# A precomputed row of expert changes in the block loop of a routed-experts stage

## The chip, the cores and the metric

The kernel runs on one core of one Trainium2 chip. The metric is the device time of one execution in microseconds (us), lower is better. Five engines work side by side on their own instruction streams: TensorE (PE, with its weight loads listed apart as PEld), VectorE (DVE), ScalarE (ACT), GpSimd (POOL) and SyncE (SP), which here only issues DMAs. They meet through semaphores. An engine's sequencer also carries out what is no tile work: waits, register arithmetic, branches, and loads of a register from memory. In the profile those carry a `q` behind the engine's name and do not count as busy.

## The reference, cut to what matters

One layer: a mixer (gated linear recurrences and chunked retention), then routed experts plus a shared expert, then a final norm. The change touches the experts alone:

```python
def swiglu(x, w_gate, w_up, w_down):
    return (jax.nn.silu(x @ w_gate) * (x @ w_up)) @ w_down

# each of 2048 tokens chooses 6 of 64 experts; tokens of one expert are packed
# into blocks of 128, every expert has at least one block
def run_block(args):
    tok, gw, e = args
    return swiglu(x[tok], w1[e], w3[e], w2[e]).astype(F32) * gw[:, None]
y = lax.map(run_block, (tok_buf, g_buf, block_expert))
routed = segment_sum(y, tok_buf)
out = routed + swiglu(x, ws1, ws3, ws2)
```

D_MODEL is 1024, the width of an expert 256, and everything is float32. How many blocks an expert has depends on the data.

## The kernel before, in words

Three stages follow each other: `front` and `mixer_out` (the mixer and the routing), `experts`, and `final`. The change lies in `experts` (from line 1826).

`experts` works through blocks of 128 tokens. Blocks 0 to 15 (NT = 16) are the shared expert over all tokens, written out in Python; blocks 16 and 17 are written out too; the rest runs in a hardware loop (`iterations`, `eng.Fori`) of two blocks a turn, on every engine. A block is a step `k`. The number of turns and the expert of a block are known only on the chip: `blocks_row` is a row of integers in on-chip memory (row 0: the expert of each block, 0 being the shared one; row 1 is filled, and nothing reads it), and `expert_of` loads one entry of it into a register (`value_load`, line 1937).

A float32 product is made of three passes with operands split into a high part (rounded by a copy on ScalarE) and a low part (the difference, on VectorE): hi x hi, hi x lo, lo x hi. So the weights of each expert have to be split as well: six pieces of 128 x 1024, four of gate and up (`split_gu` / `split`), two of down (`split_d`). The ring of raw and of split weights has two slots. The weights of expert e + 1 are split while e computes: pieces 0 to 2, then 3, in the first step of e, and the two down pieces in ScalarE's and VectorE's part `before` of the step after it. SP loads the raw pieces of expert e + 2 as soon as VectorE has split those of e (`load_free`), gate and up first, then down, in one strict order.

The order of a step `k` in the loop, engine by engine:

- PE (`step`, line 2364): gate and up, hi x hi; hi x lo; the two transposes of block k - 1's gated hidden (`ps_ht`); lo x hi; eight transposes of the gathered tokens of k + 1 (`ps_x`); then `down(k - 1)` into `ps_y`, which waits for the low part of the hidden (`ht_lo`).
- ACT (line 2136): two `change` calls, each with two `value_load`s; wait for the products of k - 1; pieces 0 to 2 if block k is the first of its expert; `copy_ht(k - 1)`; the down pieces if block k - 1 was a first one; tanh of k; `copy_xt(k + 1)`; piece 3 if k is a first one.
- DVE (line 2214): two `change` calls, four `value_load`s; pieces 0 and 1 if k is a first one; `copy_ht(k - 1)`; piece 2; gating; `copy_xt(k + 1)`; piece 3; the down pieces of `before`; `weigh(k - 1)`, which waits for the end of `down(k - 1)` (`d_done`) and multiplies `ps_y` by gate and gain.
- POOL (line 2052): gathers the tokens of k + 3 with an indirect DMA, and adds block k - 1 to the output rows in memory with an accumulating indirect DMA (`scatter`). Each scatter waits for the landing of the one before (`added`).

The order is written out by hand; no planner is involved. A "first" is computed as `(e - expert_of(k - 1)) * (NE - 1 - e)`, nonzero if the expert changed and is not the last.

Of the kernel before, what the change touches and what calls it, by code (L numbers as in the profile page):

```python
# [26 lines left out]
P = 128  # L27
# [44 lines left out]
def wait_apart(eng, semaphore, value):  # L72


    if not isinstance(value, int) or value > 0:
        eng.wait_ge(semaphore, value)
        eng.nop(nofuse=True)  # L77
# [1748 lines left out]
def experts(nc, for_dma, io, mod_d, h2_d, h2t_d, sum_d, list_d, ident, R, pre, pre_loaded, blocks_row, ends_row):  # L1826
# [12 lines left out]
    with ExitStack() as ctx:  # L1839
# [9 lines left out]
        def dma_sem(name):  # L1849
# [51 lines left out]
        sized, ordered = sem("sized"), sem("ordered")  # L1901
        block_row_done, ids_done, lists_turned, who_done, take_set, give_set = (
            sem(n) for n in "block_row_done ids_done lists_turned who_done take_set give_set".split())
        N_ROWS_DONE = 4
        added = dma_sem("added")
        clear(nc, semaphores)
        block = ctx.enter_context(nc.Block())
# [18 lines left out]
        def wait(eng, semaphore, value):  # L1926
            if not isinstance(value, int) or value > 0:
                eng.wait_ge(semaphore, value)
# [5 lines left out]
        def expert_of(eng, k):  # L1934
            if isinstance(k, int) and k <= NT:
                return int(k == NT)
            return eng.value_load(blocks_row[0:1, 0, bass.ds(k, 1)], min_val=0, max_val=NE - 1)

        def change(eng, k):

            if isinstance(k, int) and k <= NT:
                return expert_of(eng, k) + 1, k in (FIRST_SPLIT, NT)
            e = expert_of(eng, k)
            return e + 1, (e - expert_of(eng, k - 1)) * (NE - 1 - e)

        def at_change(eng, at, split, pieces):

            e, first = at
            if isinstance(first, bool):
                if first:  # L1950
                    for i in pieces:
                        split(e, i)
                return
            with eng.If(first):
                for i in pieces:
                    split(e, i)

# [143 lines left out]
        def _(act):  # L2101
# [29 lines left out]
            def copy_ht(k, par):  # L2131
                act.wait_ge(ht_done, k + 1)
                wait(act, d_done, k - 1)
                act.activation(h_t[0][:, par].bitcast(F32R), ps_t[:, 0:D_EXP], ACT.Copy).then_inc(ht_hi, 1)  # L2134

            def step(k, par, r):
                if isinstance(k, int) and k == NT + 1:
                    table(act)
                here = change(act, k)
                if not isinstance(k, int) or k > 0:  # L2140
                    before = change(act, k - 1)

                wait_apart(act, h_done, k)
                at_change(act, here, split_gu, range(3))
                if not isinstance(k, int) or k > 0:
                    copy_ht(k - 1, 1 - par)

                    wait_apart(act, d_done, k - 1)
                    at_change(act, before, split_d, range(N_GU, N_GU + N_D))
                act.wait_ge(h_done, k + 1)  # L2150
                wait(act, hg_done, k - 1)
                act.activation(th[:, par], ps_h[:, par, 0:D_EXP], ACT.Tanh, scale=0.5).then_inc(th_done, 1)  # L2152
                copy_xt(k + 1, 1 - par)
                at_change(act, here, split_gu, range(3, N_GU))
            copy_xt(0, 0)
            for i in range(N_GU):
                split_gu(0, i)
            for i in range(N_GU, N_GU + N_D):
                split_d(0, i)
            n = iterations(act, step)  # L2160
            copy_ht(n * 2 + (NT - 1), 1)

        @block.vector
        def _(dve):
# [34 lines left out]
                    c = slice(i * 512, (i + 1) * 512)  # L2199
                    dve.tensor_tensor(y[:, par, c], ps_y[:, i], g2[:, c], ALU.mult).then_inc(y_done, 1)  # L2200

            def weigh(k, par, r):

                if isinstance(k, int) and k < NT:
                    weigh_shared(k, par)
                    return
                wait(dve, added, (k - 1) * 16)
                dve.wait_ge(d_done, k + 1)
                for i in range(2):
                    c = slice(i * 512, (i + 1) * 512)  # L2210
                    dve.scalar_tensor_tensor(y[:, par, c], ps_y[:, i], gate[:, bass.ds(k, 1)], g2[:, c],  # L2211
                                             ALU.mult, ALU.mult).then_inc(y_done, 1)

            def step(k, par, r):
                if isinstance(k, int) and k == NT + 1:
                    table(dve)
                here = change(dve, k)
                before = change(dve, k - 1) if not isinstance(k, int) or k > 0 else None
                at_change(dve, here, split, range(2))
                if not isinstance(k, int) or k > 0:  # L2220
                    copy_ht(k - 1, 1 - par)
# [9 lines left out]
                if not isinstance(k, int) or k > 0:  # L2231
                    wait(dve, d_done, k - 1)
                    at_change(dve, before, split_d, range(N_GU, N_GU + N_D))
                    weigh(k - 1, 1 - par, None if r is None or (isinstance(k, int) and k == NT) else r - (1 - par))

            def sizes(tabs):

# [52 lines left out]
            def after(k):  # L2290
# [18 lines left out]
                if k == 7:  # L2309
                    dve.wait_ge(brow_done, 1)  # L2310

                    dve.tensor_copy(blocks_row[:].rearrange("p w (c k) -> p c w k", c=2),
                                    ps_r[0:1, :].rearrange("p (c w k) -> p c w k", c=2, w=2)).then_inc(rows_done, 1)
            copy_xt(0, 0)
            for i in range(N_GU):
                split(0, i)
            for i in range(N_GU, N_GU + N_D):
                split_d(0, i)
            n = iterations(dve, step, after)
            copy_ht(n * 2 + (NT - 1), 1)  # L2320
            weigh(n * 2 + (NT - 1), 1, n - 1)

        @block.tensor
        def _(pe):
# [200 lines left out]
```

## Time and profile before

| | us |
|---|---|
| median of 3 runs | 2784.51 (2784.37 to 2789.07) |
| the profiled execution | 2791.28 |
| its span, first to last instruction | 2789.4 |
| blocks 16 on (loop and its two steps ahead), span in the trace | about 1372 to 2735 |
| PE busy over the span | 2534.0 |
| DVE busy over the span | 1733.3 |
| ACT busy over the span | 1012.1 |

The profile is one execution. Busy times are sums over instructions. Waits are read from semaphore events, and each is put down to the engine whose event came last; "issue" stands for time in which the engine waited for nothing that the profile shows. The granted clock of TensorE over the span was 0.954 of full speed.

### The profile page before, as it was taken

How to read it: one execution, taken by the hardware profiler on the slowest of the kernel's cores; microseconds unless marked ns; L12 is line 12 of the kernel's file. 1: busy time of each engine (PE TensorE's matmuls, PEld its weight loads, DVE VectorE, ACT ScalarE, POOL GpSimd, SP SyncE). 2: the span in 40 equal slices, each digit the busy share in tenths (PEclk: the TensorE clock that was granted, in tenths of full speed). 3: DMA queues.
4: the chain of work that ended last, by engine and by line, in shares of the span. 5: the costliest groups of instructions: out<-in, count | busy, mean ns of one | idle time of the engine just before them, and what ended most of it. 6: DMA issues, size and time to landing. Idle time of an engine off the chain costs nothing. (4 is left out here: it accounts for less than half of the span.)

```text
span 2789.4 us, 51564 instructions
## 1 busy us (share of the span) xinstructions
PE 2534.0 (91%) x11959; PEld 2035.5 (73%) x11960; DVE 1733.3 (62%) x2732; ACT 1012.1 (36%) x1615; POOL 968.5 (35%) x1008
## 2 busy tenths in 40 slices
PE   8999999999929889849999999999999999999990
PEld 4787777776728777737887787777778777777870
DVE  4664564566325666655646757577785767768673
ACT  3221434332312222221324535254553435545352
POOL 1210025612234655531233333333333333333334
PEclk9999999999969998969999999999999999999995
DMA  7775758674565554336768969899897989979887
GB/s 280 299 274 192 267 199 301 218 282 162 190 222 200 170 166 165 119 108 165 202 173 256 265 178 284 238 265 296 242 300 189 277 256 272 292 193 289 253 233 273
DMA packets 239383, 641.94 MB, mean 230 GB/s; under 512 B 24268, under 2 KB 37904, under 8 KB 223824
## 3 DMA queue, kind: packets, MB, share of 16 engines
q1 hardware_dynamic: 188880, 459.75, 46.2%
q0 software_dynamic: 50432, 181.27, 26.9%
q8 instruction: 40, 0.66, 0.1%
q14 instruction: 31, 0.25, 0.0%
HBM read 463.61 MB, written 177.33 MB: 230 GB/s over the span
## 5 line engine op out<-in xcount | busy, mean ns | idle before, releaser
L2067 POOL DMA_INDIRECT sum_d<-w_shared_raw,give x136 | 236.7, 1741 | 647.5 <-DMA sum_d<-w_shared_raw,give 300.6
L2169 DVE TENSOR_TENSOR w_exp_lo<-w_exp,w_exp_hi (+1 forms) x256 | 307.7, 1222 | 95.5 <-ACT w_exp_hi L2108 78.4
L2337 PE MATMUL ps_h<-w_exp_hi,x_exp_t_hi 128*128 (+1 forms) x1216 | 312.8, 399 | 24.6 <-ACT w_exp_hi L2108 21.5
L2108 ACT ACTIVATE w_exp_hi<-w_exp (+1 forms) x256 | 258.5, 1054 | 179.9 <-issue 117.0
L2337 PE MATMUL ps_h<-w_exp_hi,x_exp_t_lo 128*128 (+1 forms) x1216 | 321.8, 407 | 0.0
L2337 PE MATMUL ps_h<-w_exp_lo,x_exp_t_hi 128*128 (+1 forms) x1216 | 310.5, 397 | 0.0
L2337 PEld LDWEIGHTS ps_h<-w_exp_hi,x_exp_t_hi 128*128 128x128 f32 x1216 | 229.2, 189 | 83.0 <-ACT w_exp_hi L2108 21.7
L1134 PE MATMUL ps_p<-wa_hi,hx_split 128*128 128x512 f32 x1088 | 278.9, 402 | 4.6 <-DVE kvqg_out L100 3.3
L2337 PEld LDWEIGHTS ps_h<-w_exp_lo,x_exp_t_hi 128*128 128x128 f32 x1216 | 229.7, 189 | 56.2
L2337 PEld LDWEIGHTS ps_h<-w_exp_hi,x_exp_t_lo 128*128 128x128 f32 x1216 | 217.7, 189 | 41.4
L2134 ACT ACTIVATE h_exp_t_hi<-ps_ht 128x256 fp32r<-128x256 f32 x152 | 58.1, 382 | 510.6 <-PE ps_ht L2346 502.6
L1134 PEld LDWEIGHTS ps_p<-wa_hi,hx_split 128*128 128x128 f32 x1088 | 205.4, 190 | 51.5 <-DVE kvqg_out L100 4.0
L2337 PE MATMUL ps_y<-w_exp_hi,h_exp_t_hi 128*128 (+1 forms) x608 | 205.9, 420 | 37.6 <-DVE h_exp_t_lo L2189 36.7
L2211 DVE SCALAR_TENSOR_TENSOR w_shared_raw<-ps_y,gate,g_row 128x512 f32<-128x512 f32 x272 | 191.0, 743 | 70.0 <-PE ps_y L2337 53.0
L2337 PE MATMUL ps_y<-w_exp_hi,h_exp_t_lo 128*128 (+1 forms) x608 | 193.8, 400 | 0.0
L2337 PE MATMUL ps_y<-w_exp_lo,h_exp_t_hi 128*128 (+1 forms) x608 | 193.5, 400 | 0.0
L2057 POOL DMA_INDIRECT w_shared_raw<-h_d,take x139 | 146.2, 1052 | 115.0 <-POOL take L2055 99.7
L2183 DVE TENSOR_TENSOR x_exp_t_lo<-ps_x,x_exp_t_hi 128x512 fp32r<-128x512 f32 x274 | 175.6, 682 | 0.0
L2189 DVE TENSOR_TENSOR h_exp_t_lo<-ps_ht,h_exp_t_hi 128x256 fp32r<-128x256 f32 x152 | 64.0, 421 | 148.4 <-ACT h_exp_t_hi L2134 134.3
L2337 PEld LDWEIGHTS ps_y<-w_exp_hi,h_exp_t_hi 128*128 128x128 f32 x608 | 105.9, 190 | 67.2 <-issue 46.9
L2174 DVE TENSOR_TENSOR w_exp_lo<-w_exp,w_exp_hi (+1 forms) x130 | 153.0, 1218 | 0.0
L2226 DVE SCALAR_TENSOR_TENSOR h_gated<-tanh_e,ps_h 128x256 f32<-128x256 f32 x152 | 63.6, 418 | 142.1 <-ACT tanh_e L2152 136.8
(294 smaller groups left out, 4434.9 us busy)
## 6 DMA issues: line engine op xcount, KB each, us to landing
w_exp<-in_experts SPq DMA_DIRECT2D x386, 512.0 KB
hx_split<-hx_d SPq DMA_DIRECT2D x54, 1024.0 KB, 5.4
rec_m<-rec_d SPq DMA_DIRECT2D x16, 1536.0 KB, 6.9
hx_d<-hx_split SPq DMA_DIRECT2D x18, 1024.0 KB, 6.1
wm_rest<-in_w_mod_rest POOLq DMA_DIRECT2D x16, 1024.0 KB, 5.8
rec_d<-kvqg_out SPq DMA_DIRECT2D x48, 256.0 KB, 4.3
xt<-in_xt POOLq DMA_DIRECT2D x18, 512.0 KB, 9.0
rec_d<-kt_kvf_out SPq DMA_DIRECT2D x32, 256.0 KB, 4.5
```

Of the source, the lines that this page charges most:

```text
L1134: last = pe.matmul(ps_p[:, s % 2], hx0[:, at, x, k].bitcast(F32R), wa[w][:, k, p % 2 * HD:(p % 2 + 1) * HD].bitcast(F32R), start=(m + k == ...
L2057: pool.indirect_dma_start(xg[:, par], None, h2_d[:, :], bass.IndirectOffsetOnAxis(take[:, par:par + 1], 0)).then_inc(gathered[par], 16)
L2067: pool.indirect_dma_start(sum_d[:, :], bass.IndirectOffsetOnAxis(give[:, par:par + 1], 0), y[:, par], None, compute_op=ALU.add).then_inc(a ...
L2108: act.activation(w[0][:, piece(e, i)].bitcast(F32R), raw(e, i), ACT.Copy).then_inc(gu_hi, 1)
L2134: act.activation(h_t[0][:, par].bitcast(F32R), ps_t[:, 0:D_EXP], ACT.Copy).then_inc(ht_hi, 1)
L2169: dve.tensor_tensor(w[1][:, piece(e, i)].bitcast(F32R), raw(e, i), w[0][:, piece(e, i)], ALU.subtract).then_inc(gu_lo, 1)
L2174: dve.tensor_tensor(w[1][:, piece(e, i)].bitcast(F32R), raw(e, i), w[0][:, piece(e, i)], ALU.subtract).then_inc(wd_lo, 1)
L2183: dve.tensor_tensor(x_t[1][:, par, c].bitcast(F32R), src, x_t[0][:, par, c], ALU.subtract).then_inc(xt_lo, 1)
L2189: dve.tensor_tensor(h_t[1][:, par].bitcast(F32R), ps_t[:, 0:D_EXP], h_t[0][:, par], ALU.subtract).then_inc(ht_lo, 1)
L2211: dve.scalar_tensor_tensor(y[:, par, c], ps_y[:, i], gate[:, bass.ds(k, 1)], g2[:, c], ALU.mult, ALU.mult).then_inc(y_done, 1)
L2226: own.of(dve.scalar_tensor_tensor(hg[:, par], th[:, par], 1.0, ps_h[:, par, 0:D_EXP], ALU.add, ALU.mult))
L2337: last = pe.matmul(out, x[:, j * P:(j + 1) * P].bitcast(F32R), w_part[:, bass.ds(w_at + j * stride, 512)].bitcast(F32R), start=(start and ...
```

## The change

A row of what changes at each block is made once, on VectorE after step 7: with `turn[k]` = e + 1 if block k is the first of its expert and the expert is not the last, else 0, entry k of row 1 of `blocks_row` is `turn[k - 1] * 128 + turn[k]`. ACT and DVE load this one entry a step and take it apart by `% P` and `// P` (P = 128). A zero means: nothing to split. Two more increments of `rows_done` come with it (one replaces the old one), so `N_ROWS_DONE` is 5.

The order of the loop's bodies also turns: on ACT the tanh of k - 1 and `copy_xt(k)` stand at the head of step k, behind the load, and with them piece 3 of `before`; on DVE `weigh(k - 2)` stands at the head of step k, behind the load. What was at the end of one step is at the beginning of the next, and the last ones follow the loop. PE, POOL and SP are as they were; PE still loads its own expert number twice a step.

```diff
-        N_ROWS_DONE = 4
+        N_ROWS_DONE = 5
...
-        def change(eng, k):
+        def changes(eng, k):
             if isinstance(k, int) and k <= NT:
-                return expert_of(eng, k) + 1, k in (FIRST_SPLIT, NT)
-            e = expert_of(eng, k)
-            return e + 1, (e - expert_of(eng, k - 1)) * (NE - 1 - e)
+                return tuple((0 if j not in (FIRST_SPLIT, NT) else 1 if j == FIRST_SPLIT else 2) for j in (k, k - 1))
+            both = eng.value_load(blocks_row[0:1, 1, bass.ds(k, 1)], min_val=0, max_val=NE * P - 1)
+            return both % P, both // P
...
+            def gated(k, par):
+                act.wait_ge(h_done, k + 1)
+                wait(act, hg_done, k - 1)
+                act.activation(th[:, par], ps_h[:, par, 0:D_EXP], ACT.Tanh, scale=0.5).then_inc(th_done, 1)
...
-                here = change(act, k)
+                here, before = changes(act, k)
                 if not isinstance(k, int) or k > 0:
-                    before = change(act, k - 1)
-                wait_apart(act, h_done, k)
+                    gated(k - 1, 1 - par)
+                    copy_xt(k, par)
+                    at_change(act, before, split_gu, range(3, N_GU))
                 at_change(act, here, split_gu, range(3))
...
                     at_change(act, before, split_d, range(N_GU, N_GU + N_D))
-                act.wait_ge(h_done, k + 1)
-                wait(act, hg_done, k - 1)
-                act.activation(th[:, par], ps_h[:, par, 0:D_EXP], ACT.Tanh, scale=0.5).then_inc(th_done, 1)
-                copy_xt(k + 1, 1 - par)
-                at_change(act, here, split_gu, range(3, N_GU))
...
-                here = change(dve, k)
-                before = change(dve, k - 1) if not isinstance(k, int) or k > 0 else None
+                here, before = changes(dve, k)
+                if not isinstance(k, int) or k > NT:
+                    weigh(k - 2, par)
                 at_change(dve, here, split, range(2))
...
-                    weigh(k - 1, 1 - par, None if r is None or (isinstance(k, int) and k == NT) else r - (1 - par))
+                if isinstance(k, int) and 0 < k < NT:
+                    weigh(k - 1, 1 - par)
...
-                    dve.tensor_copy(blocks_row[:].rearrange("p w (c k) -> p c w k", c=2),
-                                    ps_r[0:1, :].rearrange("p (c w k) -> p c w k", c=2, w=2)).then_inc(rows_done, 1)
+                    of_block = blocks_row[:, 0]
+                    tabs.of(dve.tensor_copy(of_block.rearrange("p (c k) -> p c k", c=2),
+                                            ps_r[0:1, :].rearrange("p (c w k) -> p c w k", c=2, w=2)[:, :, 0]))
+                    turn, last = room[0:1, 0:2 * P], slice(1, 2 * P)
+                    tabs.of(dve.memset(turn, 0.0))
+                    tabs.of(dve.tensor_tensor(turn[:, last], of_block[:, last], of_block[:, 0:2 * P - 1], ALU.subtract))
+                    tabs.of(dve.scalar_tensor_tensor(turn, of_block, float(NE - 1), turn, ALU.is_lt, ALU.mult))
+                    tabs.of(dve.scalar_tensor_tensor(turn, of_block, 1.0, turn, ALU.add, ALU.mult))
+                    dve.tensor_copy(blocks_row[:, 1, 0:1], turn[:, 0:1]).then_inc(rows_done, 1)
+                    dve.scalar_tensor_tensor(blocks_row[:, 1, last], turn[:, 0:2 * P - 1], float(P), turn[:, last],
+                                             ALU.mult, ALU.add).then_inc(rows_done, 1)
```

## Rows read from the trace of the kernel before

**Rows 1.** The page: busy time, share and instructions of two engines.

```profile
PE 2534.0 (91%) x11959; PEld 2035.5 (73%) x11960; DVE 1733.3 (62%) x2732; ACT 1012.1 (36%) x1615; POOL 968.5 (35%) x1008
```

**Rows 2.** By stretch: length; PE, PEld, DVE, ACT, POOL busy; clock, DMA share, GB/s.

```profile
1900.00:2150.00 250.00, 244.11 (x1165) 197.03 (x1164) 178.00 (x249) 115.39 (x174) 88.07 (x101) 1.00 0.89 261
```

**Rows 3.** Waits of PEld, 1400 to 2720 us: total, times, longest.

```profile
PEld ps_y L2337 <- issue: 42.9, 53, 2.6
PEld ps_h L2337 <- issue: 4.7, 8, 0.8
```

**Rows 4.** Waits of PE matmuls, the same stretch.

```profile
PE ps_y L2337 <- DVE h_exp_t_lo L2189: 30.4, 36, 2.4
```

**Rows 5.** Timeline, an even pace: two starts of a step.

```profile
2413.55 1.83 PEld L2337 LDWEIGHTS ps_h<-w_exp_hi,x_exp_t_hi 128*128 128x128 f32 x8
...
2423.08 1.83 PEld L2337 LDWEIGHTS ps_h<-w_exp_hi,x_exp_t_hi 128*128 128x128 f32 x8
```

**Rows 6.** Timeline, one step that is the first of an expert: start, duration.

```profile
1448.61 1.83 PEld L2337 LDWEIGHTS ps_h<-w_exp_hi,x_exp_t_hi 128*128 128x128 f32 x8
...
1449.21 1.41 DVE L2211 SCALAR_TENSOR_TENSOR w_shared_raw<-ps_y,gate,g_row 128x512 f32<-128x512 f32 x2 [1.36 <-PE ps_y L2337]
1449.93 2.96 ACT L2108 ACTIVATE w_exp_hi<-w_exp  x3 [3.05 <-issue]
...
1453.01 0.39 ACT L2134 ACTIVATE h_exp_t_hi<-ps_ht 128x256 fp32r<-128x256 f32 x1
1453.22 2.36 DVE L2169 TENSOR_TENSOR w_exp_lo<-w_exp,w_exp_hi  x2 [2.60 <-ACT w_exp_hi L2108]
1454.45 1.03 PEld L2331 LDWEIGHTS ps_x<-ident,w_shared_raw 128*128 128x128 f32 x8
...
1455.50 0.42 DVE L2189 TENSOR_TENSOR h_exp_t_lo<-ps_ht,h_exp_t_hi 128x256 fp32r<-128x256 f32 x1
...
1456.31 0.32 PEld L2337 LDWEIGHTS ps_y<-w_exp_hi,h_exp_t_hi 128*128 128x128 f32 x2 [0.83 <-issue]
...
1458.99 0.19 PEld L2337 LDWEIGHTS ps_h<-w_exp_hi,x_exp_t_hi 128*128 128x128 f32 x1
```

**Rows 7.** Register loads of line 1937, DVE and PE, 1400 to 2720: ns min/median/max.

```profile
L1937 DVEq TENSOR_LOAD <-blocks_row x532: 297/310/1545, 1401.7 to 2712.4; - x178
...
L1937 PEldq TENSOR_LOAD <-blocks_row x266: 296/303/1382, 1405.0 to 2718.0; - x133
```

**Rows 8.** Timeline, the fourth of four first steps in a row.

```profile
2403.28 2.35 DVE L2174 TENSOR_TENSOR w_exp_lo<-w_exp,w_exp_hi  x2
...
2405.56 1.40 DVE L2211 SCALAR_TENSOR_TENSOR w_shared_raw<-ps_y,gate,g_row 128x512 f32<-128x512 f32 x2
...
2406.88 2.34 DVE L2169 TENSOR_TENSOR w_exp_lo<-w_exp,w_exp_hi  x2
```

**Rows 9.** Waits of PEld in two windows: 1734.9 to 1758.8, 2560.6 to 2581.6.

```profile
PEld ps_y L2337 <- issue: 3.5, 2, 2.6
...
PEld ps_y L2337 <- issue: 1.9, 2, 1.0
```

**Rows 10.** Timeline around the table of step 7, and a small operation of step 5.

```profile
1287.69 0.23 DVE L2276 TENSOR_TENSOR prod<-cmp,expert_steps 128x65 f32<-128x65 f32 x1
...
1303.56 0.67 DVE L2312 CAST blocks_row<-ps_rank 1x512 int32<-1x512 f32 x1
1306.64 0.42 DVE L2189 TENSOR_TENSOR h_exp_t_lo<-ps_ht,h_exp_t_hi 128x256 fp32r<-128x256 f32 x1 [2.41 <-ACT h_exp_t_hi L2134]
```

**Rows 11.** Timeline, ACT in a step with down pieces, block after a first one.

```profile
2418.78 2.01 ACT L2112 ACTIVATE w_exp_hi<-w_exp  x2 [0.44 <-issue]
...
2420.96 1.07 ACT L2128 ACTIVATE x_exp_t_hi<-ps_x 128x512 fp32r<-128x512 f32 x2
```

**Rows 12.** Waits of POOL and DVE for the scatters, 1400 to 2720 us.

```profile
POOL sum_d L2067 <- DMA sum_d<-w_shared_raw,give: 300.6, 58, 7.3
...
DVE w_shared_raw L2211 <- DMA sum_d<-w_shared_raw,give: 8.2, 6, 1.4
```

More of the change, by code:

```diff
@@ L1937, in expert_of, with at_change @@
             return eng.value_load(blocks_row[0:1, 0, bass.ds(k, 1)], min_val=0, max_val=NE - 1)
-        def change(eng, k):
+        def changes(eng, k):
             if isinstance(k, int) and k <= NT:
-                return expert_of(eng, k) + 1, k in (FIRST_SPLIT, NT)
-            e = expert_of(eng, k)
-            return e + 1, (e - expert_of(eng, k - 1)) * (NE - 1 - e)
[L1946 to L1950, printed above, removed]
+                return tuple((0 if j not in (FIRST_SPLIT, NT) else 1 if j == FIRST_SPLIT else 2) for j in (k, k - 1))
+            both = eng.value_load(blocks_row[0:1, 1, bass.ds(k, 1)], min_val=0, max_val=NE * P - 1)
+            return both % P, both // P
+        def at_change(eng, e, split, pieces):
+            if isinstance(e, int):
+                if e:
                     for i in pieces:
@@ L1953, in at_change @@
                 return
-            with eng.If(first):
+            with eng.If(e):
                 for i in pieces:
@@ L2160, in _ @@
             n = iterations(act, step)
+            gated(n * 2 + (NT - 1), 1)
+            copy_xt(n * 2 + NT, 0)
             copy_ht(n * 2 + (NT - 1), 1)
@@ L2200, in weigh_shared, with weigh @@
                     dve.tensor_tensor(y[:, par, c], ps_y[:, i], g2[:, c], ALU.mult).then_inc(y_done, 1)
-            def weigh(k, par, r):
+            def weigh(k, par):
                 if isinstance(k, int) and k < NT:
@@ L2319, in _ @@
             n = iterations(dve, step, after)
+            weigh(n * 2 + (NT - 2), 0)
             copy_ht(n * 2 + (NT - 1), 1)
-            weigh(n * 2 + (NT - 1), 1, n - 1)
+            weigh(n * 2 + (NT - 1), 1)
         @block.tensor
```

## The prediction

> **What bounds the kernel now.** I read the page first: PE is busy 91% of the span [rows 1], so a change on the other engines can only give back time in which PE stands still. The table by stretch says the same of the block loop: PE 244.1 of 250 us, at a granted clock of 1.00, which is the 2.4 GHz level, and with the DMA engines at a share of 0.89 [rows 2]. The reader is to see two things there: PE's idle time is a few per cent, and DMA has little room.
>
> How much PE idles depends on the row one trusts. The waits of PEld in the loop are 42.9 us in 53 gaps ahead of `ps_y`, the down product, and 4.7 us ahead of `ps_h` [rows 3]; the waits of the matmuls themselves are only 30.4 us [rows 4]. I took the timeline to decide. Steps without a change of expert start 2423.08 - 2413.55 = 9.53 us apart [rows 5], and every such step looks the same. A step that is the first of its expert took 1458.99 - 1448.61 = 10.38 us [rows 6], 0.85 more, and the PEld gap in it is 0.83. So PEld's gaps are what a step loses, and the loop loses 42.9 + 4.7 = 47.6 us: the ceiling of the change. The Trainium skill ("Perfetto Trace Analysis", Per-instruction lifecycle) says that the profiler estimates where a TensorE instruction ends rather than observing it; here the trace agrees, the matmul row being short by 12 us, and by that row the sum below would be some 10 us smaller.
>
> Then, what is late in such a step? With PE's step start at 1448.61 [rows 6]: the transposes of `ps_x` are through at 1455.48, and `down` then stands until DVE's `h_exp_t_lo` (1455.50 to 1455.92). That copy is behind the two split pieces on DVE (1453.22 to 1455.58), its input from ACT was ready at 1453.40. The splits begin 2.60 us after DVE had finished `weigh` at 1450.62. The row blames ACT's `w_exp_hi`, but ACT made those from 1449.93 on, three in 2.96 us, so the first was ready at about 1450.9. What lies in the gap are the four register loads on DVE's sequencer: 532 over 133 steps, 0.31 us each by median [rows 7]; 4 x 0.31 = 1.24 us, and the arithmetic and range checks that the view of line 1937 has between them fill the rest, so that a load costs about 2.60 / 4 = 0.65 us with them. DVE's queue has nothing in it meanwhile. So the wait that ends last is the sequencer's own, and it lies between `weigh` and the splits.
>
> The Trainium skill ("Advanced Engine Details and Errata", Sequencer Loop) speaks against this reading: other engine instructions can be read and queued while the sequencer's microcode works on a control instruction. By it the loads would cost nothing, and the change would give 0. The row disagrees: the 2.60 us hold no tile work, with raw and high parts there. What the code shows is why: the splits stand in an `If` whose condition is made of the loads.
>
> **The change part by part.** Removed on DVE: three of four loads a step, and the fourth goes ahead of `weigh`'s wait for `d_done`. In [rows 6] DVE had 1.36 us idle ahead of `weigh`, waiting for PE; one load with its arithmetic is about 0.65 us, and with the turn of the loop about 1.1 us by an estimate, so it fits in. Then the splits can start when `weigh` ends, +2.0 us into the step, and end at +4.4. `h_exp_t_hi` is ready at +4.8, the low part at +5.3, and PE asks for it only at +6.87. The stall of such a step goes to zero with 1.6 us to spare; what is late next is PE itself, at 9.53 us a step. That the high pieces are there at +2.0 needs ACT earlier too: its three loads fewer and the fourth ahead of tanh let pieces 0 to 2 follow `copy_xt`, so they start 2 to 3 us earlier than 1449.93; even unmoved the first is ready at +2.3.
>
> This holds for first steps that do not follow two others. Where three or four experts of one block stand in a row, DVE has more than a step of work: six pieces at 2.35 / 2 = 1.17 us each, `weigh` 1.40, and with both copies and the gating some 2.5 more, nearly 11 us by an estimate from [rows 6, 8]. There the splits follow `weigh` with no gap (2405.56 + 1.40 against 2406.88), and `weigh` follows the down pieces (2403.28 + 2.35 against 2405.56) [rows 8]. No load is on that path, so those stalls stay. The wait view over the last two steps of each of the six such rows gives 3.5 us in the first and 1.9 in the last [rows 9], with 2.4, 2.1, 2.6 and 2.6 in between: 15.1 us. It contains the places where weight DMAs land late. The 4.7 us ahead of `ps_h` [rows 3] stay too: PE waits there for its own two loads a step, which take up to 1.38 us [rows 7] and are not touched.
>
> Sum: 42.9 - 15.1 = 27.8 us of stall that a load gates. From both sides: at most all 47.6; at least what only the pure case gives. Long loads are part of the 27.8: DVE's maximum is 1.545 us [rows 7], and four chances a step become one, ahead of a wait.
>
> Added: the table in step 7. One cast of 0.67 us becomes seven operations that each wait for the one before. The small ones of step 5 take 0.16 to 0.23 us [rows 10] for 65 elements; for 256 I take 0.4, with the wait, 7 x 0.4 = 2.8 us, 2.1 more than now. Behind the cast DVE idles 2.41 us for ACT's copy [rows 10], so 0; if that cover were gone, 2.1 us at most. Once, not per step.
>
> Moved: ACT's load now stands ahead of tanh. In a step with down pieces ACT works until 2418.78 + 2.01 = 2420.79, and tanh and `copy_xt` follow at once [rows 11]; the sequencer is free from the moment at which it handed over the second down piece, some 1 us earlier. A load with arithmetic and the loop's turn is 0.6 to 1.1 us, as on DVE, so tanh is between nothing and 0.2 us late; `copy_xt` ends at 2422.03 and PE takes its tile at 2423.08 [rows 5, 11], 1.05 us of cover. A load as long as the longest of DVE's, 1.545 us against 0.31 [rows 7], passes the cover by 0.2 to 0.4. I take 0; the far end, such a load in each of the 53 stalled steps, is 53 x 0.4 = 21 us, and the median is near the short end. `weigh`, the scatter and the gathers keep their order on their engines; the ends of the loop have the same order as before, so 0 there, give or take 0.5.
>
> Given back: the stretches with many changes get 2 to 3% faster, with DMA at 0.89. Scatters run one at a time; 58 were released by the landing of the one before [rows 12], and DVE's `weigh` waited for a scatter 8.2 us in 6 places. Saving some 1 us per pair of first steps lets such waits come up more often: I take 1 us from the sum, between 0 and 10.
>
> The forecast is 27.8 - 1 = 26.8, say 27 us. Against the profiled execution it is 2791.3 to 2764; that execution is 6.8 us above the median of the runs shown, and a span with 2 us around it. The predicted median is 2784.5 - 27 = 2757.5.
>
> **The rivals.**
>
> A: the time comes back as DMA waits. For it: the share of 0.89 [rows 2], 58 scatters bound to their predecessor [rows 12], and weights of the fourth expert in a row landing after they are wanted. Against: outside the rows of three and four PE's gaps are explained by the loads alone, and issue moves forward along with the splits. Half of the 27 would be left: 2771.
>
> B: no change. Either the load in its new place is as long as before on the same path, or the splits are late for another reason just behind it (ACT's high parts, should their loads still gate them). Against it are ACT's pieces of [rows 6], ready before the gap ends. 2784.5, within 5.
>
> C: slower, through the scatters. Place: POOL's accumulating DMA, one after another. Splits that come 2.5 us earlier put the weight loads for the next expert but one on the DMA engines 2.5 us earlier, on top of the scatter of `weigh`. POOL waits 300.6 / 58 = 5.2 us each for those of today [rows 12]. If each such scatter took a quarter of that longer, 1.3 us, and the backlog of every second one reached the loop, that is 29 x 1.3 = 38 us against the 27: 2795. It decides from the point at which a scatter lands later than two steps less a `weigh`, 2 x 9.53 - 1.40 = 17.7 us, behind its own `weigh` [rows 5, 8], since `y` has two buffers; at present DVE waits beyond it 8.2 / 6 = 1.4 us each, in 6 places.
>
> **How the numbers follow.** Forecast 0.72, A 0.14, B 0.07, C 0.07. Forecast and A are faster by over 0.2% (5.6 us, about what a measurement can tell from no change): 0.86. B is the same, 0.07; C slower, 0.07. The range: the forecast's own is from a gain of 38 (the stalls of the rows of four shrink by half too) to one of 17; A reaches to 2780. 2746 to 2780 leaves out B, C and little else.
>
> **What would show it.** The step of [rows 6] would take 9.53 us, and the DVE gap of 2.60 us ahead of its splits be under 0.3. PEld ahead of `ps_y` would sum to 14 to 18 us in the loop in place of 42.9, nearly all in third and fourth first steps, and ahead of `ps_h` 3 to 6. Loads of line 1937's kind would number about 134 on DVE and on ACT, and still 266 on PE. PE's step 8 would start on time. The prediction is wrong if gaps ahead of DVE's splits stay; if gaps ahead of `ps_h` grow (ACT's tanh and `copy_xt` late); or if DVE's waits for the scatter rise from 8 us to 20 and more.

## The result and the profile after

| | us |
|---|---|
| before, median of 4 runs | 2784.44 (2776.15 to 2789.07) |
| after, median of 4 runs | 2750.42 (2748.32 to 2753.66) |
| ratio | 0.9882, 95% interval 0.9856 to 0.9908 |
| the profiled execution after, and its span | 2748.32, 2746.5 |

The change makes the kernel 34.0 us faster; 27 were forecast, in a range from 2746 to 2780 us, which is a gain of 4.5 to 38.5. (Gains in microseconds are differences of medians, here and below, unless a ratio is named. The ratios are those on record and differ from the quotient of the medians by up to 0.0015.) The page of the kernel after, busy time of each engine (answers to [rows 1]):

```profile
PE 2512.4 (91%) x11959; PEld 2026.6 (74%) x11960; DVE 1743.4 (63%) x2738; ACT 1010.7 (37%) x1615; POOL 976.4 (36%) x1008
```

The same stretch as in [rows 2], with the same columns:

```profile
1900.00:2150.00 250.00, 247.22 (x1188) 201.48 (x1186) 180.72 (x252) 114.04 (x174) 87.14 (x102) 0.99 0.89 262
```

PE is busy 3.1 us more of the 250 and issues 23 more matmuls in them, at the same clock level and the same DMA share: the same work, closer together.

The waits in the block loop of the kernel after (engine, what it waited for, then total, times and longest; they answer to [rows 3, 12]):

```profile
POOL sum_d L2066 <- DMA sum_d<-w_shared_raw,give: 297.9, 61, 6.9
...
DVE w_shared_raw L2213 <- issue: 17.4, 20, 1.9
PEld ps_y L2351 <- issue: 15.5, 13, 2.8
...
DVE w_shared_raw L2213 <- DMA sum_d<-w_shared_raw,give: 5.7, 6, 1.4
...
DVE w_exp_lo L2171 <- ACT w_exp_hi L2107: 3.2, 10, 0.4
...
ACT w_exp_hi L2107 <- issue: 0.2, 1, 0.2
```

Ahead of `ps_y` 53 gaps have become 13. A row for `ps_h` is gone altogether. The two rows on scatters are as they were, so nothing came back there. The last row was 117.0 us before: ACT's high pieces no longer wait for its loads.

Where the 34 us lie: I measured the block loop as the distance from the first to the last of its steps' `ps_x` transposes, 136 steps. At 9.53 us a step that would be 1296 us; it was 1346.4 before and is 1313.0 after. The loop gained 33.4 us, the size of the median's gain. The two profiled executions differ by 9.6 us more, ahead of the loop, where the change has nothing (the second shared block starts at 1235.0 in one and at 1225.4 in the other), which is a difference between executions.

The step of [rows 6], the same block, in the timeline of the kernel after (start, duration):

```profile
1438.96 1.83 PEld L2351 LDWEIGHTS ps_h<-w_exp_hi,x_exp_t_hi 128*128 128x128 f32 x8
...
1439.52 1.41 DVE L2213 SCALAR_TENSOR_TENSOR w_shared_raw<-ps_y,gate,g_row 128x512 f32<-128x512 f32 x2 [1.23 <-PE ps_y L2351]
...
1440.84 2.35 DVE L2171 TENSOR_TENSOR w_exp_lo<-w_exp,w_exp_hi  x2
...
1443.78 0.42 DVE L2191 TENSOR_TENSOR h_exp_t_lo<-ps_ht,h_exp_t_hi 128x256 fp32r<-128x256 f32 x1 [0.59 <-ACT h_exp_t_hi L2133]
...
1445.81 0.30 PEld L2351 LDWEIGHTS ps_y<-w_exp_hi,h_exp_t_hi 128*128 128x128 f32 x2
...
1448.49 0.19 PEld L2351 LDWEIGHTS ps_h<-w_exp_hi,x_exp_t_hi 128*128 128x128 f32 x1
```

It takes 1448.49 - 1438.96 = 9.53 us in place of 10.38. The splits follow `weigh` with no gap where 2.60 us lay, the copy of the hidden's low part (0.42 us) starts 4.82 us into the step in place of 6.89, and `ps_y` comes without a gap.

The 13 gaps that are left, two of them in the timeline, the third and fourth of four first steps in a row:

```profile
2527.37 0.32 PEld L2351 LDWEIGHTS ps_y<-w_exp_hi,h_exp_t_hi 128*128 128x128 f32 x2 [0.87 <-issue]
...
2539.70 0.32 PEld L2351 LDWEIGHTS ps_y<-w_exp_hi,h_exp_t_hi 128*128 128x128 f32 x2 [2.77 <-issue]
```

All 13 lie in such rows, as in [rows 9]. Seven are 0.85 to 0.88 us; five are longer, to 2.77, and one is 0.23.

The register loads after (ns min/median/max) answer to [rows 7], and the table in step 7 to [rows 10]:

```profile
L1943 ACTq TENSOR_LOAD <-blocks_row x135: 273/279/820, 1367.2 to 2661.9; - x135
...
L1943 DVEq TENSOR_LOAD <-blocks_row x135: 300/317/1628, 1371.7 to 2667.1; - x135
...
L1937 PEldq TENSOR_LOAD <-blocks_row x270: 296/303/1517, 1369.1 to 2674.6; - x135
...
1293.92 0.40 DVE L2317 CAST blocks_row<-ps_rank 1x256 int32<-1x256 f32 x1
...
1296.14 0.40 DVE L2325 SCALAR_TENSOR_TENSOR blocks_row<-prod 1x255 int32<-1x255 f32 x1
1297.00 0.42 DVE L2191 TENSOR_TENSOR h_exp_t_lo<-ps_ht,h_exp_t_hi 128x256 fp32r<-128x256 f32 x1 [0.46 <-ACT h_exp_t_hi L2133]
```

One load a step on ACT and on DVE, two still on PE (these counts are over the whole trace, 135 steps with loads). The table takes 1296.54 - 1293.92 = 2.62 us, and the copy behind it still waits for ACT.

### The profile page after: what moved, and what is told of

Same layout as the page of the kernel before. It is cut to its first block and busy times, and to the rows that moved or that the text cites. A ratio compares the mean times of both kernels' runs of the same rounds, so it can differ in the third digit from the quotient of the medians.

```text
span 2746.5 us, 47753 instructions
## 1 busy us (share of the span) xinstructions
PE 2512.4 (91%) x11959; PEld 2026.6 (74%) x11960; DVE 1743.4 (63%) x2738; ACT 1010.7 (37%) x1615; POOL 976.4 (36%) x1008
## 5 line engine op out<-in xcount | busy, mean ns | idle before, releaser
L2066 POOL DMA_INDIRECT sum_d<-w_shared_raw,give x136 | 237.8, 1749 | 624.3 <-DMA sum_d<-w_shared_raw,give 297.9
L2351 PE MATMUL ps_y<-w_exp_hi,h_exp_t_hi 128*128 (+1 forms) x608 | 205.2, 419 | 18.5 <-DVE h_exp_t_lo L2191 15.2
L2127 ACT ACTIVATE x_exp_t_hi<-ps_x 128x512 fp32r<-128x512 f32 x274 | 148.4, 595 | 2.1
```

What stands on the lines that cost most here:

```text
L2066: pool.indirect_dma_start(sum_d[:, :], bass.IndirectOffsetOnAxis(give[:, par:par + 1], 0), y[:, par], None, compute_op=ALU.add).then_inc(a ...
L2127: act.activation(x_t[0][:, par, b * 512:(b + 1) * 512].bitcast(F32R), ps_x[:, b], ACT.Copy).then_inc(xt_hi, 1)
L2351: last = pe.matmul(out, x[:, j * P:(j + 1) * P].bitcast(F32R), w_part[:, bass.ds(w_at + j * stride, 512)].bitcast(F32R), start=(start and ...
```

## The experiments

**The theory:** the 42.9 us ahead of `ps_y` were DVE's four loads behind `weigh`; one load ahead of it removes them, and the order of the bodies matters little beside the number of loads. **Rivals:** the order is what pays, since it puts the load ahead of a wait; or ACT's loads are what pays. Two more questions came from the trace after: why the `ps_h` gaps went, and what holds the 15.5 us that are left.

The kernel before takes another time from one group of runs to the next (medians of 2760.59, 2762.41 and 2783.96), so only ratios within a group are compared. The last three columns are from the profiled execution.

| | median, us | before beside it | ratio (95%) | loop, us | ahead of `ps_y` | ahead of `ps_h` |
|---|---|---|---|---|---|---|
| e1, the row alone | 2733.99 | 2760.59 | 0.9894 (0.9874 to 0.9914) | 1319.6 | 18.5 | 1.5 |
| e2, the order alone | 2818.35 | 2760.59 | 1.0198 (1.0176 to 1.022) | 1401.9 | 73.2 | 29.9 |
| e3, both on DVE alone | 2732.67 | 2760.59 | 0.9896 (0.9874 to 0.9917) | 1316.1 | 16.8 | 4.9 |
| e4, both on ACT alone | 2766.01 | 2760.59 | 1.0015 (0.9999 to 1.0032) | 1349.8 | 46.3 | 5.4 |
| e5, SP's order too | 2728.86 | 2762.41 | 0.9864 (0.9843 to 0.9886) | 1308.1 | 10.5 | 2.5 |
| e6, after again | 2731.94 | 2762.41 | 0.9891 (0.987 to 0.9913) | 1308.7 | 12.6 | 0 |
| e7, after, four loads on PE | 2750.26 | 2762.41 | 0.9959 (0.994 to 0.9978) | 1336.5 | 7.8 | 44.6 |
| e8, before, four loads on PE | 2799.35 | 2762.41 | 1.0134 (1.0109 to 1.0159) | 1381.7 | 19.5 | 79.5 |
| e9, less of DVE's splits | 2741.06 | 2783.96 | 0.9853 (0.9838 to 0.9868) | 1305.2 | 0 | 9.1 |
| e10, a split on POOL | 2760.8 | 2783.96 | 0.9927 (0.9914 to 0.9941) | 1322.4 | 21.7 | 4.1 |
| e11, e5 again | 2745.55 | 2783.96 | 0.9858 (0.9844 to 0.9872) | 1307.3 | 10.6 | 1.5 |

### e1: the row alone

Table and single load as in the change; the bodies in the old order (against the kernel after).

```diff
                 here, before = changes(act, k)
-                if not isinstance(k, int) or k > 0:
-                    gated(k - 1, 1 - par)
-                    copy_xt(k, par)
-                    at_change(act, before, split_gu, range(3, N_GU))
+                wait_apart(act, h_done, k)
                 at_change(act, here, split_gu, range(3))
...
+                gated(k, par)
+                copy_xt(k + 1, 1 - par)
+                at_change(act, here, split_gu, range(3, N_GU))
...
                 here, before = changes(dve, k)
-                if not isinstance(k, int) or k > NT:
-                    weigh(k - 2, par)
                 at_change(dve, here, split, range(2))
...
-                if isinstance(k, int) and 0 < k < NT:
+                if not isinstance(k, int) or k > 0:
                     weigh(k - 1, 1 - par)
...
```

> The row and its one load a step on both engines, but the loops' bodies in the old order: the load lies where the four loads lay, between weigh and the split pieces on VectorE. Theory (the loads' length gates the splits): one load with its arithmetic and branches is about 1.0 us in place of 2.6, so the splits start about +3.0 us into the step, before the +3.7 at which the copy of the hidden's low part begins to be late; PEld ahead of ps_y 15 to 20 us in the loop, 27 to 33 us faster than before, within 3 us of the full change. Rival (it is the place that counts, the load must be ahead of the wait for down): the splits remain gated, PEld ahead of ps_y 25 us and more, half the gain or less (0 to 17 us).

0.9894 is a gain of 29.3 us at its group's 2760.6 (26.6 by the medians), and e6 has 0.9891: within the intervals the row alone is the whole change. In the profile the loop is some 6 to 11 us longer than in the kernel after (1319.6 against 1313.0 and 1308.7), with 3 to 6 us of it ahead of `ps_y`. What the order adds is at most a few us.

DVE's waits ahead of the splits that follow `weigh`, in the loop of the kernel before and then of e1:

```profile
DVE w_exp_lo L2169 <- ACT w_exp_hi L2108: 78.4, 42, 3.3
...
DVE w_exp_lo L2169 <- issue: 16.3, 10, 3.8
...
DVE w_exp_lo L2181 <- ACT w_exp_hi L2119: 8.6, 23, 0.8
DVE w_exp_lo L2181 <- issue: 7.6, 34, 1.4
```

94.7 us have become 16.2, with the one load still behind `weigh`. Directly behind `weigh`, counted over the 62 first steps of the loop, the gap was 1.53 us by mean before and is 0.14 in e1, with 0.15 at most in 42 of them and 1.41 at the longest. A look at DVE's sequencer in the step of [rows 6] tells why so little is left:

```profile
L1937 DVEq TENSOR_LOAD <-blocks_row x4: 299/302/325, 1449.8 to 1451.9; - x4
```

The first load starts at 1449.8, while `weigh` is still at work (to 1450.62), because the sequencer goes on as soon as it has handed `weigh` over. So the beginning of a chain of loads hides behind `weigh`, and a short chain hides nearly whole. What e1 doesn't part is the load itself from the arithmetic, the check and the branch that go with it: the row removes all of them together.

### e2: the order alone

The new order of the bodies with the old `change`, four loads a step (against the kernel after).

```diff
-                here, before = changes(act, k)
+                here = change(act, k)
+                before = change(act, k - 1) if not isinstance(k, int) or k > 0 else 0
...
-                here, before = changes(dve, k)
+                here = change(dve, k)
+                before = change(dve, k - 1) if not isinstance(k, int) or k > 0 else 0
```

> The new order with four loads a step at the head of the step, ahead of tanh on ScalarE and of weigh on VectorE. Theory: on VectorE 2.6 us of loads begin 1.4 us before down ends, weigh is about 1 us late and the splits start near +3.0: no stall from VectorE. On ScalarE the loads end 2.7 us after the hand-over of the last copy, later than the end of the gate and up products, so tanh and the token copy are 1 us late in plain steps (covered) and 1 to 2 us late in steps with down pieces (cover 1.05 us): gaps ahead of ps_h appear, 10 to 40 us in all. Net between 20 us faster and 10 us slower than before. Rival (place is all that counts): as fast as the full change, no gaps ahead of ps_h.

It is 58 us slower than before: the order doesn't pay by itself. My expectation, 10 us slower at most, missed this by far. The waits of its loop:

```profile
ACT tanh_e L2150 <- issue: 159.6, 96, 2.8
DVE w_shared_raw L2226 <- issue: 143.3, 80, 4.5
DVE w_shared_raw L2226 <- DMA sum_d<-w_shared_raw,give: 124.4, 45, 4.4
...
PEld ps_y L2365 <- issue: 73.2, 63, 2.5
...
PEld ps_h L2365 <- issue: 29.9, 49, 2.7
```

The first two rows have "issue" as what was waited for: the engine's own sequencer. Four loads with their arithmetic are some 2.6 us, and now tanh and `weigh` stand behind them in every step, not in first steps alone. ACT's tanh becomes late 96 times, `weigh` 80 times. The third row is the late `weigh` passed on: scatters start later, one behind another, and the next `weigh` finds its buffer still in use. With one load (the row of the kernel after above) `weigh` is late 20 times and by 17.4 us in all, which no PE row shows. So the order is safe only with the row. No run has the four loads ahead of tanh alone or ahead of `weigh` alone, so how the 58 us are shared between ACT and DVE is open.

### e3 and e4: one engine at a time

e3 has the new loads and order on DVE and the old ones on ACT; e4 the other way round. e3's edit against the kernel before:

```diff
             def step(k, par, r):        # DVE
-                here = change(dve, k)
-                before = change(dve, k - 1) if not isinstance(k, int) or k > 0 else None
+                here, before = changes(dve, k)
+                if not isinstance(k, int) or k > NT:
+                    weigh(k - 2, par)
...
```

> VectorE as in the full change, ScalarE with its four loads in the old place. Theory (the path is VectorE's): 27 to 33 us faster than before, since ScalarE's first piece is ready +2.3 us into the step and VectorE can begin at +2.0; the gap ahead of VectorE's splits is 0.3 to 0.5 us. Rival (ScalarE's late pieces gate as well): half of that, with VectorE's idle time ahead of its splits of 1 us and more, put down to ScalarE rightly.

> ScalarE as in the full change, VectorE with its four loads in the old place. Theory: within 4 us of the kernel before; ScalarE's pieces come 2 to 3 us earlier and wait, VectorE's gap of 2.6 us stays, PEld ahead of ps_y 38 to 43 us. Rival (ScalarE gates): 10 us faster and more.

DVE alone gives the whole gain (0.9896), ACT alone none (1.0015, with 1 in the interval). e4's waits:

```profile
DVE w_exp_lo L2183 <- issue: 99.6, 52, 3.7
...
PEld ps_y L2361 <- issue: 46.3, 52, 2.7
```

In e3 ACT still waits for its loads (117.0 us before), and DVE waits for ACT:

```profile
ACT w_exp_hi L2119 <- issue: 138.4, 51, 4.4
...
DVE w_exp_lo L2182 <- ACT w_exp_hi L2119: 24.7, 40, 1.9
```

DVE's 24.7 us in 40 places are ACT's late high pieces; directly behind `weigh` the gap is 0.37 us by mean over the 62 first steps, as expected. Little of it reaches PE: e3 has 16.8 + 4.9 us of gaps, the kernel after 15.5, and the loop of e3 is 3.1 us longer. So ACT's loads are a second wait, just behind DVE's own, and the path is DVE's.

e4 also corrects the reading of [rows 6]: with ACT's high pieces early, the row ahead of DVE's splits no longer blames ACT but "issue", 99.6 us in 52 places. The wait was the sequencer's all along, as the prediction had it from the sum of the loads.

### e6, e7 and e8: more loads on PE

e6 is the kernel after again, beside the others. e7 and e8 add two loads a step to PE, in the kernel after and before.

```diff
             def step(k, par, r):        # PE
+                if not isinstance(k, int):
+                    for _ in range(2):
+                        expert_of(pe, k)
                 e = expert_of(pe, k)
```

> The full change as it is, timed beside the others on one chip, for its gain with a smaller interval: 31 to 36 us faster than before.

> The full change, and TensorE's sequencer loads its expert number twice more at the head of each step (four loads a step in place of two). My prediction held that the 4.7 us ahead of ps_h are TensorE's own slow loads and stay; they went to 0 though slow loads on TensorE did not get fewer. Theory: where down is not late the sequencer is ahead of the array by more than a load, so that even 1.3 us more of loads a step hide: within 4 us of the full change. Rival (the loads are on the path, and luck took the slow ones away): 134 steps with 1.3 us more, 20 us and more slower than the full change.

> The kernel before with the same two extra loads on TensorE. Theory (a late down uses up the lead of TensorE's sequencer, then the loads at the head of the next step show): gaps ahead of ps_h in most of the steps in which down was late, 53 of them, up to 1 us each: 10 to 50 us slower than before, where the same loads cost the full change next to nothing. Rival (independent of the stall): the same cost in both kernels.

These ask why the `ps_h` gaps went although PE's loads were not touched. My expectation for e7 was under 4 us; it cost 18.3 (2750.26 - 2731.94), nearer to the rival's "20 us and more", and e8 36.9 (2799.35 - 2762.41). e7's loop:

```profile
PEld ps_h L2351 <- issue: 44.6, 68, 1.3
```

PE's sequencer runs ahead of the array, and a load is hidden as long as that lead lasts. Two loads fit in, four fit in half of the steps. The lead is consumed when `down` was late, since the sequencer then stood at that wait and has nothing queued behind it. The two traces show it step by step (counting `down` as late where PEld stood for over 0.12 us ahead of it): behind a late `down` every step has a gap ahead of `ps_h`, of 1.11 us by mean in e7 (8 steps) and 1.20 in e8 (32 steps); behind one on time 60 of 128 steps have one in e7, of 0.59 us, and 53 of 104 in e8, of 0.78. So e8 loses twice what e7 does. (The loop of e7 is 27.8 us longer than e6's and its gaps 39.8 us more, so a gap of PEld ahead of `ps_h` isn't lost to the full.) The gaps of the kernel before answer to the same reading. One of its cases, a step whose `down` is late, with the load that follows, in the view of line 1937 and in the timeline:

```profile
L1937 PEldq TENSOR_LOAD <-blocks_row x1: 1107/1107/1107, 2380.1 to 2380.1; - x1
...
2378.65 0.32 PEld L2337 LDWEIGHTS ps_y<-w_exp_hi,h_exp_t_hi 128*128 128x128 f32 x2 [0.86 <-issue]
...
2381.97 1.70 PEld L2337 LDWEIGHTS ps_h<-w_exp_hi,x_exp_t_hi 128*128 128x128 f32 x8 [0.67 <-issue]
```

And a longer load in the kernel after, in a step whose `down` was on time:

```profile
L1937 PEldq TENSOR_LOAD <-blocks_row x1: 1297/1297/1297, 1531.8 to 1531.8; - x1
...
1533.76 0.43 PEld L2351 LDWEIGHTS ps_y<-w_exp_hi,h_exp_t_lo 128*128 128x128 f32 x2
1534.23 0.90 PEld L2351 LDWEIGHTS ps_h<-w_exp_hi,x_exp_t_hi 128*128 128x128 f32 x4
```

Before, 1107 ns behind a late `down` left a gap of 0.67 us; after, 1297 ns left none. I counted PE's loads of over 0.6 us that stand between a `down` and the next `ps_h`. In the kernel before, 8 were behind a late `down` and gave the row's 8 gaps, and 6 behind one on time gave none. e4 has 8 with 8 gaps and 6 with 2 (each in the step after a stalled one). After, all 18 were behind a `down` on time and gave none. Over the ten traces with two loads a step, e2 aside, it is 20 gaps for 21 loads behind a late `down`, and 9 for 137 behind one on time. The kernel after still has 13 late ones, and that no long load met one of them is in part luck: at the rate of before (8 in 62) one or two would have.

### e5 and e11: SP's order too

SP loads the down pieces of an expert behind gate and up of the next one, in the order in which DVE frees them in rows of first steps (against the kernel after).

```diff
             with sp.Fori(2, NE // RING) as r:
                 for i in range(RING):
-                    load_free(r * RING + i, i)
+                    load_gu(r * RING + i, i)
+                    load_d(r * RING + (i - 1), 1 - i)
...
```

> The full change, and SyncE issues the gate and up pieces of expert e + 1 ahead of the down pieces of expert e (from e = 3 on). Theory: of the 15.5 us that PEld still waits ahead of ps_y in the loop, the two long gaps (2.8 us the longest) and what the last steps of rows of three and four exceed 0.9 us by are gate and up weights that land late, because their loads stand behind down loads that wait for VectorE; with the new order they are issued some 5 us earlier, gaps shrink to 0.9 us each, 9 to 12 us in all: 4 to 7 us faster than the full change, 36 to 41 faster than before. Rival (the DMA engines are full, the order does not matter): same as the full change within 2 us.

> e5 again beside the other two, for their comparison and for its own gain: 31 to 40 us faster than before.

ACT's wait for weights, e6:

```profile
ACT w_exp_hi L2107 <- DMA w_exp<-in_experts: 19.1, 18, 3.6
...
PEld ps_y L2351 <- issue: 12.6, 13, 2.1
```

and e5:

```profile
PEld ps_y L2356 <- issue: 10.5, 12, 0.9
...
ACT w_exp_hi L2116 <- DMA w_exp<-in_experts: 4.9, 4, 1.7
```

The long gaps are gone: the longest is 0.9 in place of 2.1 (2.8 in the profile of the change), so everything in the tails beyond 0.87 a step was a weight that landed late behind SP's order. What is left ahead of `ps_y` is 12 times 0.87. In time it is little: the loop of e5's profiled execution is 0.6 us shorter than e6's, since 2.1 us less ahead of `ps_y` came with 2.5 us ahead of `ps_h`. Three of these five gaps, 0.6 to 0.7 us each, are late weights again: ACT waited 1.4 to 1.7 us for one, and tanh and `copy_xt` stand behind it. By the medians e5 is 3.1 us faster than e6, 0.1%, less than the 4 to 7 expected; by the ratios it is 0.27% (0.9864 against 0.9891), and 0.24% for e11 against the change's own runs (0.9858 against 0.9882). The intervals overlap. It is the fastest version that computes everything, by a margin that the runs don't settle.

### e9: less of DVE's splits

e5 with the second down piece of the experts from 3 on split for an eighth of its width only; the rest of that low part is left out of the computation.

```diff
             def split_d(e, i):        # DVE
+                if isinstance(e, int) or i == N_GU:
+                    at = piece(e, i)
+                else:
+                    at = bass.ds(e % RING * W + i * CHUNK, CHUNK // 8)
...
```

> As e5 (the full change with SyncE's order), and of the second down piece of each expert from the third on VectorE makes the low part of one eighth of the columns only; the rest of those low parts is left out. That takes 1.0 us of VectorE's work from the step after each first step. Theory (in rows of three and four first steps VectorE's own work, 10.4 us a step, is the bound): the twelve gaps of 0.9 us each that e5 has left ahead of ps_y go, PEld ahead of ps_y under 2 us, 9 us faster than e5 in the loop. Rival (weights landing late, or ScalarE, bound those steps): the gaps stay within a third of what they are.

The gaps ahead of `ps_y` are gone altogether, so the 12 times 0.87 are DVE's amount of work in rows of first steps, as the prediction reckoned (nearly 11 us a step against 9.53). The loop is only 2.1 us shorter than e11's, where 9 were expected: other gaps came up. The waits of the loop, and one of the places in the timeline:

```profile
ACT w_exp_hi L2116 <- DMA w_exp<-in_experts: 15.5, 11, 3.0
...
PEld ps_h L2360 <- issue: 9.1, 6, 2.2
...
1741.00 1.06 ACT L2116 ACTIVATE w_exp_hi<-w_exp  x1 [0.77 <-DMA w_exp<-in_experts]
...
1742.10 0.39 ACT L2143 ACTIVATE tanh_e<-ps_h 128x256 f32<-128x256 f32 x1
1742.38 1.08 ACT L2132 ACTIVATE x_exp_t_hi<-ps_x 128x512 fp32r<-128x512 f32 x2
...
1743.74 1.70 PEld L2360 LDWEIGHTS ps_h<-w_exp_hi,x_exp_t_hi 128*128 128x128 f32 x8 [1.57 <-issue]
```

The six gaps ahead of `ps_h` lie in the six rows of three and four first steps, one in each. In all six ACT had just waited, 2.1 to 3.0 us, for gate or up weights that had not landed; tanh and `copy_xt` stand behind that piece in ACT's order, and PE waits for the copy. In e11 ACT waits 3.8 us for weights in the whole loop, here 15.5. So the rival has its part: with DVE out of the way late weights bound these rows, and 12.1 us of gaps became 9.1.

### e10: a split on POOL

e5 with the second down piece of the loop's experts split by GpSimd in place of VectorE, with a semaphore of its own.

```diff
+            def split_d1(e, i):        # POOL
+                wait_apart(pool, wd_hi, (e + 1) * N_D)
+                pool.tensor_tensor(w[1][:, piece(e, i)].bitcast(F32R), raw(e, i), w[0][:, piece(e, i)],
+                                   ALU.subtract).then_inc(wd_lo[1], 1)
...
```

> As e5, and the low part of the second down piece is made by GpSimd between its gather and its scatter, which loads the row too. Theory: if GpSimd's subtraction of 128 x 1024 takes under 4 us, VectorE is rid of 1.15 us a change and the gaps of 0.9 us go: up to 9 us faster than e5, up to 43 faster than before. Rivals: GpSimd is slow at it (over 5 us) or makes the scatters late, so that VectorE's weigh waits for them (over 30 us in the loop in place of 16): slower than e5; or its accesses slow VectorE's own instructions, seen in their mean durations (1220 ns for the pieces).

It gives back about half of the gain: 0.9927 against e11's 0.9858, 15.3 us by the medians. DVE's remaining down piece and POOL's in e10 (busy us, mean ns of one behind the count):

```profile
L2089 POOL TENSOR_TENSOR w_exp_lo<-w_exp,w_exp_hi x62 | 177.1, 2856 | 14.4 <-issue 11.5
...
L2193 DVE TENSOR_TENSOR w_exp_lo<-w_exp,w_exp_hi x62 | 144.4, 2329 | 0.0
```

DVE's pieces in e6, two an expert and 1219 ns each:

```profile
L2176 DVE TENSOR_TENSOR w_exp_lo<-w_exp,w_exp_hi x124 | 145.9, 1219 | 0.0
```

62 pieces take DVE as long as 124 did: 144.4 and 145.9 us. Two pieces that start together:

```profile
1650.06 2.40 POOL L2089 TENSOR_TENSOR w_exp_lo<-w_exp,w_exp_hi  x1
1650.06 3.47 DVE L2186 TENSOR_TENSOR w_exp_lo<-w_exp,w_exp_hi  x1
```

41 of the 62 overlap with one of POOL's pieces in time and take 2.89 us by mean; the other 21 take 1.22. Of DVE's 252 pieces of gate and up 45 overlap and take 1.64 us, the others 1.22. The sum of what the overlapping ones take above 1.22 is 88 us, against 62 x 1.22 = 76 us that DVE was spared: what is moved to POOL is more than paid for on DVE. The other rival, late scatters, is not it: `weigh` waits for them 14.3 us in e10 and 16.0 in e11. The Trainium skill ("SBUF — State Buffer", Who interferes with whom) says that a VectorE operation with both inputs in SBUF and a GpSimd operation reading SBUF contend for a port; the trace agrees, with 2.89 us against 1.22.

## Why the prediction was right, and where it wasn't

**What bounds it: right.** The gaps of PEld, and not the matmul row with its 30.4, are what the loop lost: gaps fell by 27.4 + 4.7 = 32.1 us, and the loop by 33.4.

**The cause and the mechanism: right.** The sequencer's loads between `weigh` and the splits held the step up (e3, e4), the step of [rows 6] takes 9.53 us, and its gap on DVE is gone. I placed the loads rightly but gave both halves of the change credit; e1 shows that the number of loads does nearly all of it, and the place ahead of the wait is worth a few us.

The price of a load came out right by luck. I divided the gap of 2.60 us by four. But the loads don't lie in the gap whole: they run from 1449.84 to 1452.50, 2.65 us with what belongs to them, of which 0.78 lie beside `weigh`, and 0.73 us for the branch and the hand-over of the split follow. The two errors nearly cancel: 2.65 / 4 is 0.66 us a load, and 2.60 / 4 was 0.65. What the division hid is that the gap is typically shorter (1.53 us by mean) and that a single load behind `weigh` leaves next to none (0.14 in e1). Ahead of `weigh`, where I had it fit in, the load makes `weigh` late in 20 steps, 17.4 us in all; this reached no row of PE.

**The tails, 15.1 us to stay: right, by both of their causes.** 15.5 are left. e9 shows that about 0.87 of each is DVE's work, e5 that the rest is late weights. They are two bounds close to each other: with DVE's taken away, the weights still cost 9.1 us in the same rows (e9).

**The 4.7 us ahead of `ps_h`, "PE waits there for its own two loads", "not touched": wrong.** This is the step that failed. The loads were indeed the cause, 8 long ones, and they are as long as ever (1.517 against 1.382 us at most). But they showed only where PE's sequencer had lost its lead at a late `down`. Of the late ones (62 before, 13 after, counted as in e7 and e8) most are gone, and none of those left met a long load, which is in part luck. So nothing shows. The row alone had named an instruction and not its condition; that all of its 8 gaps lay in stalled steps was there to be seen.

**Given back, 1 us: wrong in sign, by little.** DVE's wait for scatters went from 8.2 to 5.7 us, and POOL's stayed, 300.6 and 297.9. Rival A (2771) and C (2795) drew on this, and neither happened. What they described exists: e2 has it, with 124.4 us of such waits, once `weigh` itself is late in most steps. In the kernel after `weigh` comes at its old time (by mean 1.39 us behind the end of `down`, 1.40 before, 3.46 in e2), and only the splits are earlier.

**The table and ACT's load ahead of tanh, both 0: right.** The copy behind the table still waits 0.46 us for ACT. Tanh's and `copy_xt`'s cover was enough: no gap ahead of `ps_h`.

**The sum.** 27.8 were forecast from the loads, and 27.4 ahead of `ps_y` went; 4.7 more went ahead of `ps_h`, and the 1 us given back did not come: 32.1. The median moved by 34.0, and between this and 32.1 nothing is told apart: the ratio's interval is a gain of 26 to 40 us.

## What to carry to other kernels

Where a stall follows register loads on an engine, count its loads from memory, about 0.66 us each with bounds check and arithmetic here, take off what runs beside the instruction ahead of them, and first make them fewer: one table entry that holds all the answers, made once. Only then move the load ahead of a wait for another engine; four loads in that place cost 58 us. A row that names a slow instruction tells nothing of when it shows: before calling a gap untouched, look at whether it occurs only in steps that were already late.

## What the runs showed of the hardware

- PE's sequencer hides two loads a step of 9.53 us, of 0.3 us each by median and up to 1.5 (after, e6: no gap ahead of `ps_h`), but not four: 68 gaps of up to 1.3 us (e7). Behind a late `down` a load of over 0.6 us shows in 20 of 21 cases, otherwise in 9 of 137.
- Register loads of one entry, 0.3 us by median, have a tail: the longest in each of the traces is 1.2 to 1.6 us on DVE and 1.3 to 1.7 on PE. On ACT it is 0.6 to 1.5, and one load a step in place of four doesn't make it short (1.36 in e1, 1.15 in e4).
- A subtraction of two tiles of 128 x 1024 in SBUF takes VectorE 1.22 us, and GpSimd 2.40 where none of VectorE's runs beside it (12 pieces). Where they overlap in time the down pieces take VectorE 2.89 us by mean, and GpSimd's own take 2.95 (e10).
